# A ring of six split weights instead of four, with the splits moved behind the other half's steps

## What is computed

```python
for i in range(2):                            # first block
    x = x + 0.5 * rmsnorm(swiglu(rmsnorm(x, g[0]), w_in[i, 0], w_out[i, 0]), g[1])
    h = rmsnorm(x, g[2])
    m = diff_attention(h, ...) if i == 0 else s5_glu(h, ...)
    x = x + rmsnorm(m, g[3])
    x = x + 0.5 * rmsnorm(swiglu(rmsnorm(x, g[4]), w_in[i, 1], w_out[i, 1]), g[5])
    gate = sigmoid(rmsnorm(x, g[6]) @ ple_w_gate[i])
    x = x + rmsnorm(gate * (p[i] @ ple_w_proj[i]), g[7])
...                                           # second block, one layer
h = h + 0.5 * swiglu(rmsnorm(h, n1), w_ffn1_in, w_ffn1_out)
proj = rmsnorm(h, n2) @ w_in                  # window attention, HGRN2, two gates
h = h + (sigmoid(ga) * (att @ w_att) + sigmoid(gb) * (rec @ w_rec)) @ w_out
h = h + 0.5 * swiglu(rmsnorm(h, n3), w_ffn2_in, w_ffn2_out)
h = h + sigmoid(rmsnorm(h, n4) @ w_ple_gate) * (p @ w_ple_proj)
return rmsnorm(h, n5)
```

## Time and profile before

| | |
|---|---|
| median of three runs | 1752.98 us (1745.78 to 1753.33) |
| the profiled execution | 1753.75 us, its span 1752.0 us |
| mean granted TensorE clock | 0.987 |
| TensorE matmuls (PE) busy | 1686.5 us, 96% of the span, 8992 instructions |
| VectorE (DVE) busy | 1121.0 us, 64% |
| ScalarE (ACT) busy | 957.0 us, 55% |
| GpSimd (POOL) busy | 164.3 us, 9% |
| HBM traffic over the span | 168 GB/s |

### The profile page before, as it was taken

The page is one execution under the profiler, slowest core; times in us unless marked ns, Lnnn a source line. Parts: engine busy times, 40 slices in busy tenths (PEclk is TensorE's granted clock), DMA queues, the critical chain, the costliest instruction groups (busy, mean ns, idle before and its releaser), DMA issues.

```text
span 1752.0 us, 22570 instructions
## 1 busy us (share of the span) xinstructions
PE 1686.5 (96%) x8992; PEld 1420.4 (81%) x8992; DVE 1121.0 (64%) x1598; ACT 957.0 (55%) x1600; POOL 164.3 (9%) x192
## 2 busy tenths in 40 slices
PE   8999999899999999999989999999999998999997
PEld 7788799677887787878868888788889898788886
DVE  4555667679777555768666556655557685665555
ACT  5455556544567456553665555755555435455455
POOL 0000000308001102720010000100000000000000
PEclk9999999999999999999989999999999999999999
DMA  6745443454554544450445555465554323455552
GB/s 223 260 179 194 166 152 137 151 183 155 191 192 179 180 157 146 167 192 1 169 160 185 198 177 189 159 238 190 177 186 169 121 101 117 155 192 188 192 192 96
DMA packets 50201, 295.93 MB, mean 169 GB/s; under 512 B 5976, under 2 KB 12592, under 8 KB 16432
## 3 DMA queue, kind: packets, MB, share of 16 engines
q1 hardware_dynamic: 49936, 293.97, 46.8%
q0 software_dynamic: 160, 0.52, 0.1%
HBM read 293.39 MB, written 1.09 MB: 168 GB/s over the span
## 4 chain that ended last, share of the span: by engine, by line
PE 81%; DVE 8%; ACT 6%; issue 2%; DMA 2%; POOL 1%; SPq 0%; DVEq 0%; POOLq 0%; ACTq 0%
PE PS L2053 75%; DVE wlo L1276 3%; PE PS L2056 2%; ACT whi L712 2%; DMA raw<-in_w 2%; DVE wlo L1272 2%; PE PS L2259 2%; PE PS L2192 1%; ACT whi L708 1%; ACT SC L921 1%; ACT wk L744 1%; POOL st L582 0%; PE PS L2429 0%; ACT xn L786 0%; ACT wk L774 0%
## 5 line engine op out<-in xcount | busy, mean ns | idle before, releaser
L1276 DVE SCALAR_TENSOR_TENSOR wlo<-raw,ct,whi 128x512 fp32r<-128x512 f32 (+1 forms) x552 | 427.5, 818 | 282.5 <-ACT whi L712 282.5
L2053 PE MATMUL PS<-whi,xhi 128*128 128x512 f32 (+2 forms) x1328 | 516.3, 398 | 16.7 <-DVE wlo L1276 10.8
L712 ACT ACTIVATE whi<-raw,ct 128x512 fp32r<-128x512 f32 (+1 forms) x552 | 378.0, 734 | 237.5 <-PE PS L2053 198.9
L2053 PE MATMUL PS<-wlo,xhi 128*128 128x512 f32 (+2 forms) x1328 | 506.0, 390 | 0.0
L1272 DVE TENSOR_TENSOR wlo<-raw,whi 128x1024 fp32r<-128x1024 f32 x240 | 300.0, 1257 | 237.9 <-ACT whi L708 237.2
L2053 PE MATMUL PS<-whi,xlo 128*128 128x512 f32 (+2 forms) x1328 | 414.1, 390 | 3.5 <-DVE xlo L1387 3.5
L708 ACT ACTIVATE whi<-raw 128x1024 fp32r<-128x1024 f32 x240 | 251.4, 1057 | 285.3 <-PE PS L2053 204.3
L2053 PEld LDWEIGHTS PS<-whi,xhi 128*128 128x128 f32 x1328 | 251.9, 190 | 73.2 <-DVE wlo L1276 11.3
L2053 PEld LDWEIGHTS PS<-whi,xlo 128*128 128x128 f32 x1328 | 251.8, 190 | 56.2 <-DVE xlo L1387 4.3
L2053 PEld LDWEIGHTS PS<-wlo,xhi 128*128 128x128 f32 x1328 | 253.2, 191 | 47.6
L2053 PE MATMUL PS<-whi,hhi 128*128 128x512 f32 x544 | 173.7, 393 | 3.3 <-DVE hlo L1443 3.3
(11 more groups left out here) (272 smaller groups left out, 1613.0 us busy)
## 6 DMA issues: line engine op xcount, KB each, us to landing
raw<-in_w SPq DMA_DIRECT2D x263, 1024.0 KB, 4.8
gr<-in_rows SPq DMA_DIRECT2D x14, 512.0 KB, 3.7
SC<-scratch SPq DMA_DIRECT2D x1, 2048.0 KB, 10.2
SC<-scratch SPq DMA_DIRECT2D x2, 1024.0 KB, 10.2
X<-in_x SPq DMA_DIRECT2D x2, 512.0 KB, 5.5
raw<-in_w SPq DMA_DIRECT2D x2, 512.0 KB, 7.6
xn<-in_sc SPq DMA_DIRECT2D x2, 512.0 KB, 3.7
out<-xn SPq DMA_DIRECT2D x4, 256.0 KB, 2.0
```

The source lines that it names most:

```text
L712: e = a.activation(hi[:, f], src[:, f], ACT.Copy, scale=ct[:, c:c + 1])
L1276: e = v.scalar_tensor_tensor(lo[:, f], src[:, f], ct[:, c:c + 1], hi[:, f].bitcast(f32), MUL, SUB)
L2053: return pe.matmul(o, l, r, start=start, stop=stop)
```

## The change

The ring of splits gets two more places. They lie in memory that other stages use: in the turning table `rot` (places 4 and 5) and in the middle of `SC` (places 6 and 7). `slots_of` says which places half unit u may take: six with those in `rot` up to half unit 97 and from 244 on, six with those in `SC` from 98 to the beginning of step 3 of FFN 2, and the old four from there to 243. `SLOT[u]` is the place that was used longest ago, and `PREV[u]` the half unit that was in it, whose release the split waits for. `furthest` says how far `use(v)` goes: to v + 5 instead of v + 3, except for v = 0 and from step 3 of FFN 2 to the start of the GLU. At half units 98 and 244 the split also waits for the last reader of the memory that the new places take. `nil`, a small piece of `rot` that is used at the start of the kernel, moves to `wk`.

Beside this the hand-written orders change. In `start(n)` the calls of `use` that stood among the steps go: on ScalarE one `use(v0)` stands behind `squares2(k, 0)` and the load of the SiLU table, ahead of `evict_hi(k, 1)`, and the squares of half 1 stand ahead of `evict_hi(k, 0)` (in the gated case one of the two does); on VectorE `use(v0)` stands at the end. In `ple` the `use(v0)` moves on ScalarE from ahead of `evict_hi(k, 0)` to behind `projected(0)`, and on VectorE from ahead of `evict_lo(k, 0)` to behind it.

```diff
--- before.py
+++ after.py
@@ -168,6 +168,28 @@
             pass
 
 
+TURNS_FROM, TABLES_FROM, TURNS_TO = FFN_AT[1], up_at(2, 3), GLU_AT + 4
+
+
+def slots_of(u):
+
+    if u < TURNS_FROM or u >= TURNS_TO:
+        return range(NSPLIT + 2)
+    return (0, 1, 2, 3, 6, 7) if u < TABLES_FROM else range(NSPLIT)
+
+
+SLOT, PREV, last_in = [], [], {}
+for u in range(N_HALF):
+    SLOT.append(min(slots_of(u), key=lambda i: last_in.get(i, -1)))
+    PREV.append(last_in.get(SLOT[u], -1))
+    last_in[SLOT[u]] = u
+
+
+def furthest(v):
+
+    return v + (AHEAD if v < 1 or TABLES_FROM <= v <= GLU_AT else AHEAD + 2)
+
+
 class Ahead:
 
 
@@ -175,7 +197,7 @@
         self.n, self.done = 0, -1
 
     def upto(self, v):
-        while self.n <= min(v + AHEAD, N_HALF - 1) and (self.n < NSPLIT or self.n - NSPLIT <= self.done):
+        while self.n <= min(furthest(v), N_HALF - 1) and PREV[self.n] <= self.done:
             self.n += 1
             yield self.n - 1
 
@@ -201,7 +223,9 @@
         xlo = sb("xlo", [128, 8, S], f32r)
         hhi = sb("hhi", [128, 4, S], f32r)
         hlo = sb("hlo", [128, 4, S], f32r)
+        rot_at = nc.sbuf_base
         rot = sb("rot", [128, 2, 32, NCH])
+        w_rot = nc.alloc_sbuf_tensor_at("w_rot", [128, 4, HU], f32r, offset=rot_at)
         wk = sb("wk", [128, 4 * S])
         sg = wk[:, 0:2 * S].rearrange("p (f t) -> p f t", f=2)
         hf = wk[:, 2 * S:4 * S].rearrange("p (f t) -> p f t", f=2)
@@ -215,7 +239,11 @@
         snkt = sb("snkt", [128, 8])
         s_eo = sb("eo_t", [128, 64])
         SW = 21248
+        sc_at = nc.sbuf_base
         SC = sb("SC", [128, SW])
+        w_sc = nc.alloc_sbuf_tensor_at("w_sc", [128, 4, HU], f32r, offset=sc_at + 4 * 2560)
+        slots = [(whi[:, i, :], wlo[:, i, :]) for i in range(NSPLIT)]
+        slots += [(a[:, 2 * i, :], a[:, 2 * i + 1, :]) for a in (w_rot, w_sc) for i in range(2)]
         PS = ctx.enter_context(nc.psum_tensor("PS", [128, 8, 512], f32))
 
         st_at = [0]
@@ -380,7 +408,7 @@
         decay = wk.rearrange("p (i n) -> p i n", i=16)
         r_tmp = SC[:, kb_at - 1024:kb_at].rearrange("p (i n) -> p i n", i=32)
         zc = stat()
-        nil = rot[:, 0, 0:2, :].rearrange("p i n -> p (i n)")
+        nil = wk[:, 0:128]
 
 
         cut = Cut()
@@ -701,9 +729,14 @@
                         q.wait_ge(s_raw[u // 2 % NRAW], 16 * (u // 2 // NRAW + 1))
                     else:
                         q.wait_ge(s_first, 16)
-                    if u >= NSPLIT:
-                        q.wait_ge(s_used, u - NSPLIT + 1)
-                    hi, src = whi[:, u % NSPLIT, :], raw[:, u // 2 % NRAW, u % 2 * HU:u % 2 * HU + HU]
+                    if PREV[u] >= 0:
+                        q.wait_ge(s_used, PREV[u] + 1)
+                    if u == TURNS_FROM:
+                        q.wait_ge(a_add, 8)
+                        q.wait_ge(a_sc, 8)
+                    if u == TURNS_TO:
+                        q.wait_ge(s_st, 7)
+                    hi, src = slots[SLOT[u]][0], raw[:, u // 2 % NRAW, u % 2 * HU:u % 2 * HU + HU]
                     if u not in G_COLS:
                         a.activation(hi, src, ACT.Copy).then_inc(s_hi, 1)
                         continue
@@ -733,15 +766,17 @@
             def squares(k, h):
                 if k not in POST:
                     return
-                ss, y, sc = ss1[k][h], y_of(k, h), 1 / (32 * W_OF[k])
-                q.wait_ge(s_sq, n_sq(k, h, 0) - 1)
-                for i, f in enumerate((LO, HI)):
-                    if k in GATED:
-                        q.wait_ge(s_gated, n_part(k, h, i))
-                    else:
-                        y_ready(q, k, h, i == 0)
-                    q.wait_ge(s_sq, n_sq(k, h, i) - 1)
-                    a.activation(wk[:, f], y[:, f], ACT.Square, scale=sc, accum_out=ss[:, i:i + 1]).then_inc(s_sq, 1)
+                for i in range(2):
+                    square(k, h, i)
+
+            def square(k, h, i):
+                ss, y, sc, f = ss1[k][h], y_of(k, h), 1 / (32 * W_OF[k]), (LO, HI)[i]
+                if k in GATED:
+                    q.wait_ge(s_gated, n_part(k, h, i))
+                else:
+                    y_ready(q, k, h, i == 0)
+                q.wait_ge(s_sq, n_sq(k, h, i) - 1)
+                a.activation(wk[:, f], y[:, f], ACT.Square, scale=sc, accum_out=ss[:, i:i + 1]).then_inc(s_sq, 1)
 
             def sigmoid(k, h):
                 for i, f in enumerate((LO, HI)):
@@ -816,18 +851,16 @@
                     sigmoid(k, 0)
                     squares(k, 0)
                     sigmoid(k, 1)
-                    use(v0 - 1)
+                    square(k, 1, 0)
                     evict_hi(k, 0)
-                    use(v0)
-                    squares(k, 1)
+                    square(k, 1, 1)
                 else:
                     squares(k, 0)
+                    squares(k, 1)
                     evict_hi(k, 0)
-                    use(v0 - 1)
-                    use(v0)
-                    squares(k, 1)
                 squares2(k, 0)
                 load_table(ACT.Silu)
+                use(v0)
                 evict_hi(k, 1)
 
             def ffn(n):
@@ -1265,9 +1298,8 @@
             def use(u0):
                 for u in ahead.upto(u0):
                     q.wait_ge(s_hi, u + 1)
-                    hi = whi[:, u % NSPLIT, :]
+                    hi, lo = slots[SLOT[u]]
                     src = raw[:, u // 2 % NRAW, u % 2 * HU:u % 2 * HU + HU]
-                    lo = wlo[:, u % NSPLIT, :]
                     if u not in G_COLS:
                         v.tensor_tensor(lo, src, hi.bitcast(f32), SUB).then_inc(s_lo, 1)
                         continue
@@ -1411,20 +1443,17 @@
                     add_x(k, 0)
                     gated(k, 1, 1)
                     evict_lo(k, 0)
-                    use(v0 - 1)
-                    use(v0)
                     gated_times_g(k, 1)
                 else:
                     gate_or_low(k, 0)
                     times_g(k, 0)
                     add_x(k, 0)
-                    use(v0 - 1)
-                    evict_lo(k, 0)
-                    use(v0)
                     gate_or_low(k, 1)
                     times_g(k, 1)
+                    evict_lo(k, 0)
                 add_x(k, 1)
                 evict_lo(k, 1)
+                use(v0)
 
             def ffn(n):
                 k = 2 * n
@@ -2057,7 +2086,7 @@
 
             def weight(u):
                 q.wait_ge(s_lo, u + 1)
-                return whi[:, u % NSPLIT, :], wlo[:, u % NSPLIT, :]
+                return slots[SLOT[u]]
 
             def run(parts, base, last, by_half=None, finish=None, step=2, between=None):
```

## The result

The changed kernel takes 1760.93 us (median of five, 1758.0 to 1763.26), the kernel before 1748.17 us (median of five, 1745.78 to 1753.33). The ratio is 1.0061 [1.0043, 1.0079]: it is slower, by just over the 0.5% that tells from no change. The forecast was 1751.0 us and no change that can be told.

The account below looks back on a forecast made before the run. TensorE's streaming products were taken to bound the kernel (81% of the chain). Terms 2.7 + 6.6 - 5 + 0 - 7.5 - 2.0 + 3.2 = -2.0 gave 1751.7 us, 1751.0 against the median; range 1740 to 1761.

Parts of the forecast that it names:

- Ring and orders at the starts: Second to fifth `start`: X and half 1 earlier, partly lost to a late SiLU; sum -7.5 us, bounds -11.5 and -3.
- Start of the kernel: First SiLUs stand behind a split waiting for its transfer; hidden turn +4.4 us, net +2.7, bounds 0 and +6.
- First start with a post norm: Layer 1's second FFN: X about 5 us earlier, wait moves from a split to the hidden turn; -5 us, bounds -3 and -11.
- Turning table: Around 430 to 437 us, GpSimd's table: `hlo` stays, TensorE arrives earlier and waits longer; 0, bounds -4 and +1.6 us.
- Plain splits: Before and in the output projections: three waits of 2.0 us in all, cured by depth; -2.0 us.
- Ple: Three `ple` stages: two more splits in front of evict_hi(k,1), not covered; +2.2 us each, +6.6 in all.
- the rule that the whole prediction used: ScalarE and VectorE queues: deeper splits keep position and wait for the same product; weights are just 5.5 us further ahead.
- Slots and guards: Added waits at half units 98 and 244 name work done by then, `nil` serves only the start: 0, covered.
- rival B: Late transfers at six FFN starts, 7.5 instead of 5.0 us as requests bunch: +15 us, about 1766; chance 0.12.
- The clock: Slow clock behind new waits at the kernel's start and each `ple`: four times 1.6 us by a half, +3.2 us.

Follow-up runs that it names:

- the first experiments: Follow-up runs that began with the kernel before, unchanged, measured and profiled once more: 1748.11 us, ratio 1.0001.
- R: Changed kernel, with SyncE asking for weights two half units further ahead only in front of the rows of gains: 1751.57 us, ratio 1.0020 to the kernel before.

## Why the prediction was wrong

The sum was -2.0 us and the trace has +11.6. Two steps of it failed: the GLU, which it put at nothing and which cost 8.1 us, and `ple`, where it had 9.0 us with the clock and the trace has 13.6. The time of 1760.93 us still lies just inside the stated range of 1740 to 1761. That is luck, since the base was off too: the three times that were shown have a median of 1752.98 us, the 17 runs beside the first experiments one of 1748.27, which put the forecast time 4.7 us too high and hid a third of the error. By its steps:

- *Ring and orders at the starts* (-1.6, -2.8, -1.5, -1.6): measured -1.0, -1.9, -3.6, -1.8. Right in kind and in sum; in the third 1.7 us are a fall of the clock that the kernel before happened to have, and without them it is -1.9.
- *Start of the kernel* (+2.7): the wait of 3.91 us at the hidden turn, behind a split that waited 4.06 us for its transfer, is there; +2.5 to the end of the attention. Right in the mechanism. That the sizes agree is partly luck: 1.7 of the 2.5 us are slow clock, which the sum had in another term.
- *First start with a post norm* (-5): the wait changed its name as forecast (4.44 us for the hidden turn), and GpSimd's clear is what makes it. Measured -3.4: right in kind, within the bounds, and 1.7 us of it are clock. The Trainium skill (SBUF — State Buffer, Who interferes with whom) says that tensor_scalar can take the port pair that GpSimd and VectorE share, and that an operation with two SBUF inputs contends only with a GpSimd operation that reads SBUF. The trace agrees: the three tensor_scalars took 5.16 us beside the clear, a split with two SBUF inputs beside it 0.71.
- *Turning table* (0): `hlo` 3.85 instead of 2.0 and 1.8 us. Right.
- *Plain splits* (-2.0): -2.1. Right.
- ***Ple*** (+2.2 each): the two splits do cost 2.1 us each, but the first two stages wait 3.0 and 3.1 us more than before. What is over, about 1 us, is a transfer: with SyncE ahead at the rows (R) the waits are 3.15 and 3.16 instead of 4.09 and 4.22 us. The step that failed is the rule that the whole prediction used, "in steady state nothing else on ScalarE or VectorE moves in time". It looked at the splits' position in two queues and not at the third: SyncE's list asks for weights at places of its own, with `AHEAD = 3` in it, and a row holds it back there. The larger part of the miss is the price of the clock, below.
- ***Slots and guards*** ("0, covered"): I checked the two waits that the code adds and not the step from 3 to 5 ahead that `furthest` makes at half unit 241, in the middle of the GLU. The ring has to pull in one transfer more than TensorE uses, just where a row holds back SyncE. It cost 8.1 us, the largest term, and the sum had none. This is rival B's mechanism, a split that waits for its transfer ahead of a step of the main chain, at another place. B's condition, transfers that land later because requests come in a bunch (7.5 instead of 5.0 us), was met where it counted: all transfers took 4.8 us in the median as before, but those behind the rows took 6.6 us in two `ple` stages and 6.6 and 8.3 us in the GLU. They were asked for late as well. B had 0.12; it expected this at the starts of all six FFNs, and there the sum came out without it.
- *The clock* (+3.2): behind each of the three `ple` waits of 3.1 to 4.2 us the granted clock fell:

```profile
543.00:553.00 10.00, 9.09 (x33) 7.38 (x34) 4.25 (x6) 6.24 (x12) 1.70 (x4) 0.83 0.46 146
1101.00:1111.00 10.00, 9.30 (x35) 7.55 (x36) 4.37 (x5) 6.04 (x12) 1.70 (x4) 0.83 0.43 146
1726.00:1736.00 10.00, 9.98 (x37) 8.19 (x38) 3.04 (x3) 5.59 (x10) 1.70 (x4) 0.83 0.06 21
```

  10 x 0.17 = 1.7 us each, where the sum had a half of 1.6. Behind the waits of 1.1 us in the kernel before the same windows show 1.00. So each us of new wait in the first `ple` cost about 1.6 us ((3.0 + 1.7) / 3.0). The price was the upper of my two. The Trainium skill (TensorE: Matmul & The Clock Gate, What's actually happening) says that throttled is the default state and activity releases it; the three windows agree.

## What to carry to other kernels

A ring between a loader and a consumer is as deep as the list of whoever feeds it. When a stage is allowed further ahead, move every queue upstream by as much, and look for each place where an ordered queue holds a request back behind something else (here a row that waits for a norm). A large transfer directly behind another lands later (6.6 instead of 4.8 us behind a row of half its size). And the step to a greater depth is itself a burst of transfers: put it where nothing of the main chain stands behind it, and in small steps, which helped at the kernel's start, the one place where they were tried.

Two late things in front of one step hide each other. An edit that gives nothing alone (old `ple` order: the same waits in two of three stages) isn't refuted until the other is gone; it was worth 11.5 us then.

## What the runs showed that I had not expected

- The same kernel, with waits of TensorE that differ by 0.6 us in sum, differs by 7.4 us between two profiled executions, through the granted clock (0.89 or 1.00 in the 15 us after a wait of 2.91 us). In the `ple` stages of all 17 traces the granted clock of the 10 us behind the wait was 1.00 after each of 26 waits of 1.1 us, and between 0.69 and 0.86 after 21 of 22 waits of over 3 us. Elsewhere a short wait doesn't exclude a fall: the first profile of the kernel before has one at 790.2 us, behind waits of 1.10 and 0.82 us, and the second has none there.
- Two parts that are each slower alone (ring 1.0142, orders 1.0107) are less slow together (1.0061), and with 2 further half units in SyncE's list and the old `ple` order faster than the start (0.9956).
- The memset of 8192 elements stretches three VectorE tensor_scalars of 32 elements from 0.18 us each to 5.16 us together at one place and 6.58 us at another.
